# Expert rows scaled on leaving PSUM, both picks gathered with an add onto the h rows, a plain one-hot for the last expert, and rows turned with a column stride

## The chip, the cores and the metric

One NeuronCore of one Trainium2 chip runs one program. The metric is the device time of one execution in microseconds (us). PE is the matrix engine, DVE the vector engine, ACT the scalar engine, POOL the general engine, SP the engine that issues most transfers. Each reads its own instructions in order, and semaphores tie them together.

## The reference

520 tokens (512 of a prompt, 8 samples), 1024 wide, float32. Only the second half of the layer is touched here:

```python
h = layer_norm(ALPHA * x + m, ln1_g, ln1_b)          # m: the token mixer's output
probs = softmax(h @ router_w + router_b)             # 16 experts in 4 groups of 4
# the best group by the sum of its two largest; its two largest are the picks
weights = sel_v / jnp.sum(sel_v, axis=-1, keepdims=True)
for e in range(N_EXPERTS):
    u = jax.nn.silu(t @ w_gate[e]) * (t @ w_up[e])
    out = out + gates[:, e:e + 1] * (u @ w_down[e])
y = layer_norm(ALPHA * h + f, ln2_g, ln2_b)
```

## The kernel before

Every float32 matrix is split in a rounded high part (ACT writes it, for expert weights into `ring`) and a low part (the difference, by POOL for the mixer and by DVE for the experts), and a product is three matmuls: high by high, high by low, low by high. Up to about 690 us the mixer runs so. Then `h` is written to DRAM (`h_rows`) and the experts follow.

An expert takes up to C = 96 tokens. A small product `find_ids` of a one-hot (`mark` on DVE builds it from the token's position in the expert, `posm`) with `id_cols` gives the ids of its tokens, DVE adds them up (`take_ids`), POOL gathers the rows of `h` (`hs`), PE turns them (`turn`, 8 transposes), ACT and DVE split them (`tokens_in`, `tokens_low`). Then come the products gate, up and down, 24 matmuls each. ACT copies the expert's rows out of PSUM (`rows_out`, tile `y_out`) and SP stores them in `y_rows`. Experts are run in the order `TURN`; `each_tile` writes the first and the last three by hand (m = 0, 13, 14, 15) and puts m = 1 to 6 in a loop that runs twice. In the loop DVE, ACT and PE work on three experts at once: in step m PE does gate(m), `find_ids` for m + 2, the turn of u(m-1) and of the rows of m + 1, up(m), down(m-1).

The gate is applied at the end, per token. `h` is loaded back (`h_back`), POOL gathers each token's first pick into `y_a` (the picks in the first 12 experts: `slot_early`) and its second pick into `y_b` (`slot_ready`), and DVE forms `y_a * weight + h_back` (`partial`). Rows of the last expert don't go through DRAM for prompt tokens: PE adds them from `y_last_hi` and `y_last_lo` with a weighted one-hot `share_hi`, `share_lo` (`share_last`), on top of `y_a` that it brings into PSUM by the identity. The 8 sample tokens are spread over 128 partitions (16 per token, 64 wide: `sy_a`, `sy_b`, `sh_back`) and always gathered, so their second gather waits until the last expert's rows are stored (`half_stored`). `results` on DVE then adds `y_b` with its weight, takes mean and variance with ACT (`deviation`) and normalises four blocks of 128 tokens and the samples. In DRAM the rows of `h` lie with even and odd columns apart, so that `turn` reads runs of 128 columns.

A token count over 96 for an expert leads to further passes, behind a branch on `n_max`. These inputs don't take it.

## Time and profile before

| | |
|---|---|
| three runs | 1028.72, 1028.82, 1029.62 us (median 1028.82) |
| the profiled execution | 1029.47 us, of it 1027.7 us span |
| PE, DVE, ACT, POOL busy | 97%, 77%, 47%, 37% |
| mean granted clock of PE | 0.993 |
| mixer, experts, end | to about 690, 714 to 1002, 1002 to 1027.7 us |

The span runs from the first to the last instruction; 1.77 us lie around it. Times in rows are from the span's start.

### The profile page before, as it was taken

What the parts mean: (1) busy time and instruction counts of PE and PEld (TensorE: products, weight loads), DVE (VectorE), ACT (ScalarE), POOL (GpSimd) and SP (SyncE); (2) the same over time, 40 slices, a digit from 0 to 9 for tenths busy, and PEclk for the clock granted to TensorE, in tenths of its full rate; (3) what the DMA queues carried; (4) which work ended last, traced back from release to release, by engine and by line L of the source; (5) the groups of instructions that cost most, each with busy time, mean ns of one, the idle gap of its engine ahead of it and who ended that gap; (6) DMA issues with size and microseconds to landing.
All of it is one profiled execution on the core that took longest, in us unless ns stands there. A gap on an engine that the chain in (4) does not pass through costs nothing.

```text
span 1027.7 us, 19645 instructions
## 1 busy us (share of the span) xinstructions
PE 999.9 (97%) x7246; PEld 904.1 (88%) x7246; DVE 793.4 (77%) x982; ACT 478.5 (47%) x674; POOL 379.0 (37%) x278
## 2 busy tenths in 40 slices
PE   7999999999999999999999999998999999999995
PEld 7999999999999999999999999986677777777773
DVE  4598889888989985844434498237989898999987
ACT  4232322223232335134442323452788887878765
POOL 3444444444454755344544454320200000000355
PEclk9999999999999999999999999998999999999998
DMA  7432323233232222333235522647999999999475
GB/s 219 120 103 82 102 82 97 86 88 95 85 99 82 82 83 73 101 111 91 82 102 162 186 82 92 257 154 286 398 389 397 391 399 389 399 391 399 155 247 179
DMA packets 147290, 190.55 MB, mean 185 GB/s; under 512 B 6819, under 2 KB 114339, under 8 KB 147228
## 3 DMA queue, kind: packets, MB, share of 16 engines
q1 hardware_dynamic: 140107, 176.74, 49.4%
q0 software_dynamic: 3008, 10.55, 3.2%
q10 hardware_dynamic: 4129, 2.67, 0.9%
q8 instruction: 26, 0.43, 0.2%
q14 instruction: 20, 0.16, 0.1%
HBM read 179.16 MB, written 11.76 MB: 186 GB/s over the span
## 4 chain that ended last, share of the span: by engine, by line
PE 91%; DVE 5%; issue 2%; DMA 2%; ACT 1%; POOL 0%; SPq 0%; DVEq 0%; POOLq 0%; ACTq 0%
PE pr L1079 60%; PE pr L1269 16%; PE work L1269 8%; DMA sb_tok<-in_state_conv_b_dram 1%; PE work L1245 1%; PE work L1161 1%; PE pr L1310 1%; PE pr L1289 1%; DMA hs<-h_rows,ids 0%; PE work L1186 0%; DVE y_a L2015 0%; PE work L1087 0%; PE pr L1234 0%; DVE q_hi L1596 0%; PE pr L1178 0%
## 5 line engine op out<-in xcount | busy, mean ns | idle before, releaser
L595 POOL TENSOR_TENSOR w_lo<-raw,w_hi 128x512 fp32r<-128x512 f32 x208 | 297.2, 1449 | 326.8 <-ACT w_hi L724 326.8
L1079 PE MATMUL pr<-x_hi,w_hi 128*128 128x260 f32 x1264 | 255.2, 283 | 0.0
L1079 PE MATMUL pr<-x_hi,w_lo 128*128 128x260 f32 x1264 | 254.8, 283 | 0.0
L1079 PE MATMUL pr<-x_lo,w_hi 128*128 128x260 f32 x1264 | 254.3, 283 | 0.0
L728 ACT ACTIVATE ev<-pr 128x520 f32<-128x520 f32 x96 | 58.2, 606 | 372.7 <-PE pr L1079 372.7
L1079 PEld LDWEIGHTS pr<-x_hi,w_hi 128*128 128x128 f32 x1264 | 195.0, 189 | 0.3
L1079 PEld LDWEIGHTS pr<-x_hi,w_lo 128*128 128x128 f32 x1264 | 194.9, 188 | 0.0
L1079 PEld LDWEIGHTS pr<-x_lo,w_hi 128*128 128x128 f32 x1264 | 194.3, 188 | 0.0
L1522 DVE SCALAR_TENSOR_TENSOR work<-b_pad,par,work 128x512 f32<-128x512 f32 x224 | 148.1, 742 | 0.0
L724 ACT ACTIVATE w_hi<-raw 128x512 fp32r<-128x512 f32 x208 | 118.9, 622 | 3.7 <-DMA raw<-in_w_in_dram 3.4
L632 POOL DMA_INDIRECT hs<-h_rows,ids x15 | 19.3, 1288 | 247.5 <-DVE ids L1801 247.5
L1269 PE MATMUL pr<-ring,hs_hi 128*96 128x512 f32 x246 | 97.8, 398 | 0.0
L1269 PE MATMUL pr<-ring,hs_lo 128*96 128x512 f32 x246 | 96.8, 393 | 0.0
L1705 DVE TENSOR_TENSOR w_up_lo<-w_up,ring 128x1024 fp32r<-128x1024 f32 x64 | 75.2, 1219 | 19.0 <-ACT ring L868 19.0
L868 ACT ACTIVATE ring<-w_gate 128x1024 fp32r<-128x1024 f32 x64 | 67.8, 1062 | 23.3 <-PE pr L1269 10.6
L1705 DVE TENSOR_TENSOR w_down_lo<-w_down,ring 128x1024 fp32r<-128x1024 f32 x64 | 75.3, 1214 | 1.7 <-ACT ring L868 1.7
L1705 DVE TENSOR_TENSOR w_gate_lo<-w_gate,ring 128x1024 fp32r<-128x1024 f32 x64 | 75.4, 1215 | 0.8 <-ACT ring L868 0.7
L1582 DVE TENSOR_TENSOR ev<-ev,ev 128x520 f32<-128x520 f32 x16 | 11.9, 744 | 79.4 <-ACT ev L728 79.4
L868 ACT ACTIVATE ring<-w_down 128x1024 fp32r<-128x1024 f32 x64 | 65.7, 1053 | 4.7 <-PE pr L1269 4.0
L868 ACT ACTIVATE ring<-w_up 128x1024 fp32r<-128x1024 f32 x64 | 62.4, 1046 | 2.1 <-PE pr L1261 1.9
L1269 PEld LDWEIGHTS pr<-ring,hs_lo 128*96 128x96 f32 x246 | 39.7, 161 | 17.3
L1269 PEld LDWEIGHTS pr<-ring,hs_hi 128*96 128x96 f32 x246 | 39.8, 162 | 16.0
(397 smaller groups left out, 1749.7 us busy)
## 6 DMA issues: line engine op xcount, KB each, us to landing
raw<-in_w_in_dram SPq DMA_DIRECT2D x80, 512.0 KB, 3.7
w_gate<-in_expert_w_gate_dram SPq DMA_DIRECT2D x16, 2048.0 KB, 14.4
w_up<-in_expert_w_up_dram SPq DMA_DIRECT2D x16, 2048.0 KB, 13.0
w_down<-in_expert_w_down_dram SPq DMA_DIRECT2D x16, 2048.0 KB, 12.5
y_rows<-y_out SPq DMA_DIRECT2D x14, 384.0 KB
raw<-in_w_a_out_dram SPq DMA_DIRECT2D x8, 512.0 KB, 4.1
raw<-in_w_c_out_dram SPq DMA_DIRECT2D x8, 512.0 KB, 4.1
raw<-in_w_b_out_dram SPq DMA_DIRECT2D x8, 512.0 KB, 3.9
```

The source lines that it names most:

```text
L595: pool.tensor_tensor(w_lo[:, slot, k], raw[:, slot, k], w_hi[:, slot, k].bitcast(F32), ALU.subtract).then_inc(w_split, 1)
L632: pool.indirect_dma_start(out=hs[:], out_offset=None, in_=h_rows, in_offset=bass.IndirectOffsetOnAxis(ap=ids[:, m % 2:m % 2 + 1], axis=0)) ...
L724: act.activation(w_hi[:, slot, k], raw[:, slot, k], ACT.Copy).then_inc(w_rounded, 1)
L728: act.activation(out, src[:, :, 0:HALF], func).then_inc(evacuated, 1)
L868: act.activation(rounded(kind, i, last, opening, slots), chunk(kind, s, i), ACT.Copy).then_inc(ps.hi[kind], 1)
L1079: mm = pe.matmul(pr[slot][:, h, 0:HALF], w[:, slot, k, :], x[:, k, h * HALF:(h + 1) * HALF], start=(k == 0 and w is w_hi and x is hi), sto ...
L1161: mm = pe.matmul(work[TILE[f"sp{q}"]][:, i, c * P:(c + 1) * P], vt[:, c, g * P:(g + 1) * P], ws_t[:, g, :], start=True, stop=True)
L1245: mm = pe.transpose(work[0][:, k // 4, k % 4 * C:(k % 4 + 1) * C], source[:, (k % 2 * 4 + k // 2) * P:(k % 2 * 4 + k // 2 + 1) * P], ident ...
L1269: mm = pe.matmul(out(h), x[:, k, :], w[:, cols], start=(k == 0 and x is hi and w is w_hi_i), stop=(k == k_of * CH - 1 and x is lo))
L1522: do(dve.scalar_tensor_tensor(acc, b_pad[:, k:k + TP], col(j, R_CONVB + k), acc, ALU.mult, ALU.add))
L1582: do(dve.tensor_tensor(gate[:], gate[:], prod[:], ALU.mult))
L1705: dve.tensor_tensor(chunk(kind, s, i, w_e_lo), chunk(kind, s, i), rounded(kind, i, last, opening, slots).bitcast(F32), ALU.subtract).then_ ...
```

## The change

1. **Gate at PSUM.** `find_ids` multiplies the one-hot by `slot_cols`, five columns for each expert: the two of `id_cols` and three bfloat16 parts of the token's weight for that expert. `next_gate` on ACT adds the three parts into a column of `gate`, and `rows_out` copies with `scale=gate`. The gates of the first two experts come from `find_gates` on PE, which takes the place of eight filler transposes (`keep_busy(8)`), and `first_gates` on ACT.
2. **Gathers that add.** Each gather adds its rows to `h_back` in place (`compute_op=ALU.add`), the early one once `h_back` is loaded, the second one once the first has landed (`y_in`). A pick that isn't to be added points at row 0 of `y_rows`, a row of zeros that a new transfer writes near the start. `partial` and all that belongs to it is gone.
3. **Plain one-hot.** `share` is turned and copied once during expert 15 and has no weight and no low part; `share_last` has two matmuls for each half block where it had four, and takes the first halves of blocks 0 to 2 first.
4. **Column stride.** Rows of `h` lie in DRAM in their natural order, and `turn` reads every second column.
5. In `normalised` one dummy Sqrt on ACT moves behind the branch.

The core of the diff (the further pass, renames and declarations left out):

```diff
@@ SP @@
+            sp.wait_ge(x_split, 1)
+            sp.dma_start(y_rows[0:1, :].rearrange("o (a b) -> o a b", b=16), b_pad[0:1, 0:16].unsqueeze(1).to_broadcast([1, D // 16, 16])).then_inc(h_stored, 16)
             sp.dma_start(sb_tok[:], state_conv_b[0].rearrange("(b s) k n -> (s k) b n", b=2)).then_inc(states_in, 16)
@@ POOL @@
+            def fetch(b, slot, table):
+                pool.indirect_dma_start(out=h_back[:, b, :], out_offset=None, in_=table,
+                                        in_offset=bass.IndirectOffsetOnAxis(ap=slot[:, b:b + 1], axis=0), compute_op=ALU.add).then_inc(y_in[b], 16)
...
-            pool.wait_ge(first.done["down"], (E - 1) * CH)
-            fetch(y_a, slot_early, y_a_in, y_rows[0:EARLY * C, :])
-            pool.wait_ge(end_dve, 2)
+            pool.wait_ge(back_in, 32)
+            for b in range(4):
+                fetch(b, slot_early, y_rows[0:EARLY * C + 1, :])
+            pool.wait_ge(end_dve, 3)
...
-                fetch(y_b, slot_ready, y_b_in, y_rows[0:(E - 1) * C, :])
+                for b in range(4):
+                    pool.wait_ge(y_in[b], 16)
+                    fetch(b, slot_ready, y_rows[0:(E - 1) * C + 1, :])
+                pool.wait_ge(y_in[4], 16)
                 pool.wait_ge(first.half_stored, 32)
@@ ACT @@
+            def gate_in(ps, src, m):
+                act.activation(gate_parts[:, m % 2], src, ACT.Copy, accum_out=gate[:, m % 6:m % 6 + 1]).then_inc(ps.gates_in, 1)
+            def first_gates(ps, q):
+                act.wait_ge(ps.gates_mm, q + 1)
+                for j in range(2):
+                    gate_in(ps, pr[1][0:C, 1, 8 + 3 * j:11 + 3 * j], j)
+            def next_gate(ps, m, t):
+                act.wait_ge(ps.ids_ready, t + 4)
+                act.wait_ge(ps.gates_in, t + 2)
+                if m:
+                    act.wait_ge(ps.y_ready, t)
+                gate_in(ps, pr[1][0:C, 1, 2:5], m + 2)
...
                     if m < 15:
                         tokens_in(ps, m + 1, t + 1)
+                    if m <= 13:
+                        next_gate(ps, m, t)
@@ PE @@
-                    mm = pe.matmul(pr[1][0:C, 1, 0:2], onehot[:, b, :], id_cols[:, b, :], start=(b == 0), stop=(b == NTB - 1))
+                    of = id_cols[:, b, :] if x is None else slot_cols[:, b, bass.ds(x, 1), :].rearrange("p o n -> p (o n)")
+                    mm = pe.matmul(pr[1][0:C, 1, 0:2 if x is None else 5], onehot[m % 2][:, b, :], of, start=(b == 0), stop=(b == NTB - 1))
...
-                    mm = pe.transpose(work[0][:, k // 4, k % 4 * C:(k % 4 + 1) * C], source[:, (k % 2 * 4 + k // 2) * P:(k % 2 * 4 + k // 2 + 1) * P], ident[0:C, 0:C])
+                    mm = pe.transpose(work[0][:, k // 4, k % 4 * C:(k % 4 + 1) * C], of_pair[:, k // 2, k % 2, :], ident[0:C, 0:C])
...
                 turn(ps, n0)
-                if ps is first:
-                    keep_busy(8)
+                find_gates(ps, n0)
@@ DVE @@
+                if ps is first:
+                    spread_weights()
...
-                low_parts(ps, "down", 0, t, (3,), last=True)
                 if ps is first:
                     spread_samples()
-                    share_marks()
-                    partials(16)
+                low_parts(ps, "down", 0, t, (3,), last=True)
+                if ps is first:
+                    share_low(0)
+                    share_low(1)
...
-                    step(dve.scalar_tensor_tensor(z_tile[b][:], wide(y_b[:, b, :]), s_wm[:, b:b + 1], z_tile[b][:], ALU.mult, ALU.add,
+                    step(dve.scalar_tensor_tensor(z_tile[b][:], other, 1.0, whole, ALU.mult, ALU.add, accum_out=agg[:, s, 0:1]))
```

How the instructions stand on an engine, at the three places that the prediction speaks of. First ACT, from the last chunk of the first expert's gate matrix on. Before:

```order
L868 ACTIVATE ring<-w_gate_74 128x1024 [waits first_gate_in0,h_stored]
L891 ACTIVATE hs_hi<-work 128x768 [waits first_turned]
L868 ACTIVATE ring<-w_up_77 128x1024 [waits first_gate_done,first_up_in0]
L868 ACTIVATE ring<-w_up_77 128x1024 [waits first_gate_done]
L922 ACT_TABLE_LOAD [waits first_u]
```

With the change:

```order
L875 ACTIVATE ring<-w_gate_74 128x1024 [waits first_gate_in0,h_stored]
L905 ACTIVATE gate_parts,gate<-pr 96x3 [waits first_gates_mm]
L905 ACTIVATE gate_parts,gate<-pr 96x3
L898 ACTIVATE hs_hi<-work 128x768 [waits first_turned]
L875 ACTIVATE ring<-w_up_77 128x1024 [waits first_gate_done,first_up_in0]
```

Two small instructions, with a wait on PE's `find_gates`, now stand ahead of the rows' high part. Second PE in the loop, between gate and the turn of u. Before:

```order
L1231 REGISTER_ALU
L1234 MATMUL pr<-id_cols,onehot 96x2 [waits first_ids_ready,first_onehot]
L1234 MATMUL pr<-id_cols,onehot 96x2 x4
L1308 ISA
L1310 MATMUL pr<-ident,u 128x96 [waits first_u]
```

With the change:

```order
L1259 REGISTER_ALU
L1263 ISA [waits first_ids_ready,first_onehot]
L1263 MATMUL pr<-slot_cols,onehot_183 96x5
L1263 ISA
L1263 MATMUL pr<-slot_cols,onehot_183 96x5
L1263 ISA
L1263 MATMUL pr<-slot_cols,onehot_183 96x5
L1263 ISA
L1263 MATMUL pr<-slot_cols,onehot_183 96x5
L1263 ISA
L1263 MATMUL pr<-slot_cols,onehot_183 96x5
L1347 ISA
```

The wait moved from a matmul to a register instruction ahead of it (ISA: it computes the address of the expert's columns), and each of the five matmuls has such an instruction. Third ACT at the end, the two halves of the last expert's rows. Before:

```order
L907 ACTIVATE y_last<-work 96x512 [waits first_down_done]
L911 ACTIVATE share_hi<-pr 96x512 [waits end_mm]
L912 ACTIVATE y_last_hi<-work 96x512
L914 DMA y_rows<-y_last 96x512 [waits first_half_ready]
L907 ACTIVATE y_last<-work 96x512 [waits first_down_done]
L912 ACTIVATE y_last_hi<-work 96x512
L914 DMA y_rows<-y_last 96x512 [waits first_half_ready]
```

With the change:

```order
L934 ACTIVATE y_last_hi<-work,gate 96x512 [waits first_down_done,first_gates_in]
L936 ACTIVATE y_last<-work,gate 96x512 [waits end_dve]
L938 DMA y_rows<-y_last 96x512 [waits first_half_ready]
L934 ACTIVATE y_last_hi<-work,gate 96x512 [waits first_down_done]
L936 ACTIVATE y_last<-work,gate 96x512 [waits end_dve]
L938 DMA y_rows<-y_last 96x512 [waits first_half_ready]
```

`y_last`, which is what gets stored, is now written last of the two, after DVE has formed the low part (`end_dve`).

## Rows read from the trace of the kernel before

**Rows 1.** The page: span, and the chain that ended last by engine.

```profile
span 1027.7 us, 19645 instructions
PE 91%; DVE 5%; issue 2%; DMA 2%; ACT 1%; POOL 0%; SPq 0%; DVEq 0%; POOLq 0%; ACTq 0%
```

**Rows 2.** The chain in order of time (start, us, what), one expert apart.

```profile
929.13 0.18 PE pr L1234 x5
...
947.00 0.18 PE pr L1234 x5
```

**Rows 3.** The same chain near the start.

```profile
15.22 0.39 SPq L425
...
15.65 11.39 DMA sb_tok<-in_state_conv_b_dram
```

**Rows 4.** Timeline, first expert (start, us, engine, line, operation, [idle before <-releaser]).

```profile
711.96 1.14 PE L1245 MATMUL work<-ident,hs 96*128 96x96 f32 x8 [0.24 <-DMA hs<-h_rows,ids]
...
713.14 0.81 ACT L891 ACTIVATE hs_hi<-work 128x768 fp32r<-128x768 f32 x1 [8.51 <-PE work L1245]
```

**Rows 5.** Timeline, ACT: the smallest reading of PSUM with a sum.

```profile
1016.31 0.31 ACT L1001 ACTIVATE y_b<-pr,s_agg 128x64 f32<-128x64 f32 x1
```

**Rows 6.** Timeline, one expert of the loop.

```profile
941.56 1.02 ACT L900 ACTIVATE y_out<-work 96x1024 f32<-96x1024 f32 x1 [1.78 <-PE work L1269]
...
945.84 0.65 DVE L1794 TENSOR_TENSOR onehot<-ev,router 128x480 bf16<-128x480 f32 x1
...
946.84 0.34 PE L1234 MATMUL pr<-id_cols,onehot 128*96 128x2 bf16 x5
```

**Rows 7.** Line 1794: register instructions of DVE (x, min/median/max ns).

```profile
L1794 DVEq FUSED_REGOPS  x12: 64/64/81, 729.4 to 926.7; - x12
```

**Rows 8.** Timeline, the same expert, further on (DVE).

```profile
950.95 0.15 DVE L1801 TENSOR_REDUCE ids<-pr 96x1 int32<-96x2 f32 x1
```

**Rows 9.** Timeline, the last expert's products and rows.

```profile
998.37 0.16 DVE L1942 COPY s_spread<-pr 128x5 f32<-128x5 f32 x1
...
999.99 0.64 PE L1374 MATMUL pr<-ident,share_tok 128*96 128x128 f32 x4 [0.48 <-DVE share_tok L1955]
...
1002.05 0.59 ACT L907 ACTIVATE y_last<-work 96x512 f32<-96x512 f32 x1 [0.31 <-PE work L1302]
...
1002.68 0.32 ACTq L914 DMA_DIRECT2D y_rows<-y_last  x1
...
1004.07 0.68 DVE L1977 TENSOR_TENSOR y_last_lo<-work,y_last_hi 96x512 fp32r<-96x512 f32 x1
```

**Rows 10.** Timeline, POOL's second gathers and DVE after them.

```profile
1000.83 1.74 POOL L677 DMA_INDIRECT y_b<-y_rows,slot_ready  x1 [0.82 <-DVE slot_ready L1961]
...
1008.30 2.02 POOL L682 DMA_INDIRECT y_b<-y_rows,s_idx  x1 [0.30 <-issue]
...
1006.76 1.29 DVE L2006 SCALAR_TENSOR_TENSOR pr<-y_b,s,pr 128x1024 f32<-128x1024 f32 x1 [0.82 <-PE pr L1387]
...
1008.22 1.27 DVE L1967 SCALAR_TENSOR_TENSOR y_a<-y_a,s,h_back 128x1024 f32<-128x1024 f32 x1
...
1014.65 1.28 DVE L2015 SCALAR_TENSOR_TENSOR y_a<-work,agg,ln_rows 128x1024 f32<-128x1024 f32 x1
```

**Rows 11.** Transfers issued in 1000 to 1002.5, 1002.5 to 1005 and 1008 to 1012 us (last: us to landing).

```profile
y_rows<-y_last ACTq DMA_DIRECT2D x1, 192.0 KB, 2.1
...
y_b<-y_rows,slot_ready POOLq DMA_INDIRECT x1, 5.5
...
y_rows<-y_last ACTq DMA_DIRECT2D x1, 192.0 KB, 4.2
...
y_b<-y_rows,s_idx POOLq DMA_INDIRECT x1, 4.6
```

**Rows 12.** Busy time by stretch (PE, PEld, DVE, ACT, POOL, granted clock, DMA share, GB/s).

```profile
706.00:712.00 6.00, 4.95 (x29) 4.47 (x28) 2.58 (x16) 0.00 (x0) 2.02 (x2) 0.50 0.43 130
...
1003.00:1012.00 9.00, 8.99 (x28) 5.14 (x29) 7.96 (x12) 6.04 (x9) 6.41 (x4) 1.00 0.84 259
```

More of the change, by code:

```diff
@@ L265, in build @@
         u_lo = place("u_lo", "par", [P, FB, C], F32R)
-        onehot = place("onehot", "acc_a", [P, NTB, C], BF16)
+        onehot = [place(f"onehot{i}", "acc_a", [P, NTB, C], BF16, plus=i * NTB * C * 2) for i in range(2)]
+        slot_cols = place("slot_cols", "rw", [P, NTB, E, 5], BF16)
         iota = ev[4][:, 0:C]
@@ L324, in build @@
         more_posm = sem("more_posm")
[L325 to L326 removed]
+        y_in = [sem(f"y_in{b}") for b in range(NTB)]
+        cols_ready = sem("cols_ready")
         y_read = sem("y_read")
@@ L553, in _ @@
                 sp.wait_ge(first.half_stored, 32)
-                sp.wait_ge(partial_ready, NTB)
+                for b in range(NTB):
+                    sp.wait_ge(y_in[b], 16)
                 sp.wait_ge(end_mm, 6)
@@ L1351, in step @@
                     if m <= 13:
-                        find_ids(ps, t + 2)
+                        find_ids(ps, m, t + 2, expert(2))
                     if m:
@@ L1384, in part @@
                     cols = slice(h * D // 2, (h + 1) * D // 2)
-                    pe.matmul(z_tile[b][:, h, :], ident[:], y_a[:, b, cols], start=True, stop=False)
-                    for w, y in ((share_hi, y_last_hi), (share_lo, y_last_hi), (share_hi, y_last_lo)):
-                        mm = pe.matmul(z_tile[b][:, h, :], w[:, n], y[:, cols], start=False, stop=y is y_last_lo)
-                    return mm
-                pe.wait_ge(end_dve, 5)
-                pe.wait_ge(partial_ready, 1)
-                part(0, 0)
-                pe.wait_ge(end_dve, 6)
-                part(0, 1).then_inc(end_mm, 1)
-                for b in (1, 2, 3):
-                    pe.wait_ge(partial_ready, b + 1)
-                    part(b, 0)
-                    part(b, 1).then_inc(end_mm, 1)
+                    for y in (y_last_hi, y_last_lo):
+                        mm = pe.matmul(z_tile[b][:, h, :], share[:, n], y[:, cols], start=y is y_last_hi, stop=y is y_last_lo)
+                    return mm
+                for h in range(2):
+                    pe.wait_ge(end_act, 2 + h)
+                    pe.wait_ge(end_dve, 4 + h)
+                    for b in range(3):
+                        mm = part(b, h)
+                        if h:
+                            mm.then_inc(end_mm, 1)
+                pe.wait_ge(first.half_ready, 2)
+                part(3, 0)
+                part(3, 1).then_inc(end_mm, 1)
             pe.sem_inc(first.turned, 1)
@@ L1964, in partial @@
-            def partial(b, landed):
-                dve.wait_ge(y_a_in[b], landed)
-                to = y_a[:, b, :] if landed == 16 else z_tile[b][:].rearrange("p h t -> p (h t)")
-                dve.scalar_tensor_tensor(plain(to), plain(y_a[:, b, :]), s_wa[:, b:b + 1], paired(h_back[:, b, :]), ALU.mult,
-                                         ALU.add).then_inc(partial_ready, 1)
-            def sample_partial(landed):
-                dve.wait_ge(y_a_in[4], landed)
-                dve.scalar_tensor_tensor(plain_s(sy_a), plain_s(sy_a), s_spread[:, 3:4], paired_s(sh_back), ALU.mult, ALU.add).then_inc(partial_ready, 1)
```

257 lines of the change are left out of this document (118 added, 139 removed).

## The prediction

> **What bounds the kernel now.** I read the page first: PE holds 91% of the chain that ended last, DVE 5% [rows 1]. The chain in order of time then shows what that means for an expert: the same group of five small matmuls returns after 17.87 us (947.00 less 929.13), and between the two the chain never leaves PE [rows 2]. So in the loop any time that PE loses is lost, and nothing that DVE, ACT or POOL save is gained. Two stretches are different. At the start the chain runs through SP: a weight load is issued at 15.22, `sb_tok` 0.43 us later, and its landing releases PE [rows 3]. When the first expert begins, ACT stands 8.51 us until the first rows are turned, and PE's first gate matmul hangs on ACT's high part [rows 4]. At the end, from 1002 us, PE has little to do, and DVE, ACT, the gathers and the last stores set the pace [rows 9, 10].
>
> The change works at all of these places, so I go through it in order of time. Its sum is made against the profiled execution, 1029.47 us, which is 0.65 above the median of the three runs, 1028.82; I add the sum to the median.
>
> **The zero row.** SP issues one more transfer between the weight load and `sb_tok`. Neighbours in that queue stand 0.43 us apart [rows 3], it is on the chain, and PE has no slack behind it: **+0.45 us** (0.3 if it issues like a small one, 0.7 if 64 pieces of 64 bytes take longer than one plain block).
>
> **The first two gates.** `find_gates` can't start before the turn (PE in order); its inputs on DVE, nine small operations after the second ids, end while the rows are still on their way, since ACT has 8.51 us of waiting there [rows 4]. Ten small matmuls take twice a group of five (0.18 us in the chain, 0.34 with the last one's end [rows 2, 6]), some 0.45 us; they replace eight fillers, so PE issues no more than before. But ACT now waits for them and then does two readings with a sum before `hs_hi`. The nearest row is 0.31 us for 64 columns [rows 5]; three columns may take 0.25. 0.4 + 2 x 0.27 = **+0.95 us** on the path to the first gate matmul (0.7 to 1.3). What follows is paced by PE and moves with it.
>
> **In the loop, PE.** `find_ids` keeps five matmuls with five columns in place of two; nothing by itself. But its columns are now found by a register, and ahead of each of the five stands a register instruction; the first of them holds the wait for the one-hot, so PE's sequencer stops there instead of running ahead. The one-hot is ready at 946.49 (945.84 + 0.65), 0.35 us before PE takes the group up at 946.84 [rows 6]. `y_out`, now with a scale from memory, may add up to 0.1 to ACT and so to the one-hot, which stands behind ACT's `ring` for up. A register instruction for the same purpose took DVE 64 ns [rows 7]. Five of them, with 0.04 us for each matmul (0.18 / 5), are 0.5 us from 946.55, so the last matmul goes out at about 947.05 where before all five had gone at 947.02, and the turn of u waits for one register instruction more. At 64 ns I get some 0.1 us lost, at twice that 0.35. No row shows PE's own register instructions. I take 0.15 for each of twelve looped experts: **+1.8 us**, bounds 0 (the sequencer is fast enough) and 4.2.
>
> **In the loop, the rest.** ACT gets `next_gate`, about 0.3 us, and has to wait for DVE's ids (951.1 [rows 8]), about 1.2 us later than it would come to it. ACT sits 1.78 us before `y_out` in every expert [rows 6] and also waits for PE between the chunks of `ring`, so it has caught up by then: **0**, and up to +0.2 per expert if that cover is gone. `y_out` needs the gate two experts later: no wait. The turn reads columns 8 bytes apart. No row has PE reading so; the nearest is DVE, whose operations on `y_a` with every second column took 1.27 us against 1.28 and 1.29 for plain ones [rows 10]. I take **0**; if the turn took half as long again (eight in 1.14 us, at a clock not yet full [rows 4]), 16 experts would add 9 us.
>
> The Trainium skill ("SBUF — State Buffer", section "Door 1: The DMA port swizzle") says that memory is read in lines of 16 bytes, at full rate with at least two hits in a line, which four-byte elements at a step of two still have. By it the turn costs nothing, the same as my 0.
>
> **Expert 15.** The four transposes of the one-hot, with the 0.48 us that PE waited for DVE [rows 9], leave the space between the last products; the transposes come back before `up_last`, with a copy of 0.6 us on ACT ahead of the store and the last down chunks, and the samples' indices (0.35 us from 998.37) now stand ahead of DVE's last low part. About 0.9 goes and 0.75 comes: the last product ends as before, near 1002 us, and the first half 0.9 later than before.
>
> **The last store.** Per half ACT writes `y_last_hi` (0.59), DVE `y_last_lo` (0.68), then ACT `y_last` (0.59) and its store [rows 9]. ACT is through with the first half at about 1002.8, and with the second 2.0 later: the second store goes out at 1004.75 instead of 1002.68. Stores of this form took 2.1 and 4.2 us [rows 11]; with gathers beside it I take 4.2: landed at 1009.0.
>
> **The gathers.** The samples' index no longer waits behind the one-hot's arithmetic, so the second gathers start at about 999.8 instead of 1000.83 [rows 10], if the early ones have landed. The first lands 5.5 us later [rows 11], 1005.3; PE, with eight matmuls less in front, is ready by 1004.8. DVE then starts adding at 1005.3 instead of 1006.76, and needs the samples 7.9 us less two partials (1.27 and 0.3) later, at 1011.5. But the samples' second gather waits for the last store, 1009.0 (before it began at 1008.30), and takes 4.6 us [rows 10, 11]: 1013.6, and the block after it starts at 1013.85 instead of 1014.65. What follows is as before. **-0.8 us**, bounds: -3.1 if the samples are not late, -0.1 if the store is 0.7 slower. One table load less on ACT lies beside DVE's work and gives nothing.
>
> A gather that adds must read `h_back` too. No row has one. Below: nothing extra. Above: twice the time of the engines. I take **+0.5**.
>
> **The sum:** 0.45 + 0.95 + 1.8 - 0.8 + 0.5 = +2.9 us, so 1028.82 + 2.9 = **1031.7 us**.
>
> **Rivals.**
>
> *Register instructions are covered.* If PE's sequencer loses nothing in the loop, the sum is +1.1: 1029.9 us. For it: other register instructions already stand in PE's loop, some with a wait, and the chain shows PE without a gap [rows 2]. Against: the wait now stops the sequencer, 0.35 us before the matmuls are due.
>
> *The adding gathers double.* From 1003 to 1012 the transfer engines are busy 84% [rows 12]. If adding rows double that work, 7.6 us become about 13, and the samples land near 1017 instead of 1013: +3.4 on the forecast's other terms, 1034.6 us with the loop's loss and 1032.8 without. The Trainium skill ("Collectives: The Full Stack", section "The bandwidth ceiling: the fold count and why AG ≠ RS ≠ AR") says that a reduce in the transfer engines costs two source reads and so halves the rate. That rule speaks against the change, and would give this case; no run here shows it yet. The early gathers, which begin only once `h_back` is in, would also end later.
>
> *Faster.* If the last store lands in 2.1 us, the samples are gathered right behind the other rows and DVE is the bound: -3.1 at the end. Adding is free and the register instructions are covered: 0.45 + 0.95 - 3.1 = -1.7, 1027.1 us. It decides at the samples' landing: only before about 1011.5 us, and with the head's 1.4 us cut to under 1, is the kernel faster by over 0.2%.
>
> *The clock.* PE ran at half its clock (1.2 GHz) from 706 to 712 us, after little work [rows 12]. The new 1.4 us gap behind the turn may bring that back: a third of an expert (one product, 17.87 / 3 = 6 us [rows 2]) at half clock costs 6 us more, of which 2 to 5 would show: 1034 to 1037.
>
> *The column stride costs PE*, as above: 1041.
>
> **How the numbers follow.** 0.2% (2.1 us) is about what can be told from no change. The forecast, a loss in the loop of 0.05 to 0.35 per expert with gathers that cost little: 0.36. Covered registers, gathers cheap: 0.26. Doubled gathers: 0.14. Clock or stride: 0.08. Faster end: 0.16, of which about 0.13 beyond 0.2% when I count what no row shows. Slower by over 0.2% (above 1030.9) is two thirds of the first, most of the doubled ones and the clock, a fifth of the second, 0.52; the same 0.34; faster 0.14. The range reaches from the faster end to the doubled gathers: 1027.0 to 1035.0.
>
> **What would show it.** The start of `sb_tok`'s issue at 16.1 instead of 15.65; ACT's `hs_hi` of the first expert 1.4 us after the turn's end rather than at once; one expert of the loop at 18.0 instead of 17.87 us; the stride: time from `find_ids` to the up product grown by more than the register instructions explain; the second half's store at 1004.8 relative to a last product at 1002; the landing of gathers near 5.5 us. I would be wrong above all if PE's loop period doesn't move, if the adding gathers take much longer than plain ones, or if the samples are no longer what DVE waits for.

## The result: 1.7% slower

| kernel | median of its runs | ratio to before |
|---|---|---|
| before, beside it | 1029.22 us (4 runs, 1028.72 to 1029.88) | |
| changed | 1046.71 us (4 runs, 1045.62 to 1047.37) | 1.0168, 95% interval 1.0151 to 1.0186 |

The forecast was 1031.7 us in a range that ended at 1035.0. The loss is 17.5 us of medians, and 17.9 us between the two profiled spans (1045.6 and 1027.7 us). Between the profiled spans it came in three stretches: about 3.7 us at the start of the first expert and the turn behind it (the forecast had 0.95 there), 9.6 us from the first looped expert to the last expert's first product (it had 1.8), and 5.7 us behind the last product (it had 0.3 less than before). Expert 15 gained 0.8 us, and the first turn began 0.4 us earlier.

The first lines of the page of the changed kernel; PE holds the chain almost as before (90% and 91%, [rows 1]):

```profile
span 1045.6 us, 19709 instructions
PE 90%; DVE 4%; issue 3%; DMA 1%; ACT 1%; POOL 0%; ACTq 0%; SPq 0%; DVEq 0%; POOLq 0%
```

### The profile page after: what moved, and what is told of

Its sections match the earlier page's. It is cut to its first block, busy times and chain, and to the rows that moved or that the text cites. A ratio compares the mean times of both kernels' runs of the same rounds, so it can differ in the third digit from the quotient of the medians.

```text
span 1045.6 us, 19709 instructions
## 1 busy us (share of the span) xinstructions
PE 1003.2 (96%) x7224; PEld 909.4 (87%) x7224; DVE 791.8 (76%) x969; ACT 478.1 (46%) x703; POOL 368.0 (35%) x278
## 4 chain that ended last, share of the span: by engine, by line
PE 90%; DVE 4%; issue 3%; DMA 1%; ACT 1%; POOL 0%; ACTq 0%; SPq 0%; DVEq 0%; POOLq 0%
PE pr L1107 59%; PE pr L1308 16%; PE work L1308 8%; PE work L1284 1%; DMA sb_tok<-in_state_conv_b_dram 1%; PE work L1189 1%; PE pr L1263 1%; PE pr L1349 1%; PE pr L1328 1%; DMA hs<-h_rows,ids 0%; PE work L1214 0%; DVE y_a L2024 0%; PE work L1115 0%; DVE q_hi L1635 0%; PE pr L1206 0%
## 5 line engine op out<-in xcount | busy, mean ns | idle before, releaser
L631 POOL DMA_INDIRECT hs<-h_rows,ids x15 | 13.9, 929 | 265.8 <-DVE ids L1853 250.7
L1308 PEld LDWEIGHTS pr<-ring,hs_lo 128*96 128x96 f32 x246 | 40.0, 162 | 17.5
```

The lines of the kernel that those rows point to most:

```text
L631: pool.indirect_dma_start(out=hs[:], out_offset=None, in_=h_rows, in_offset=bass.IndirectOffsetOnAxis(ap=ids[:, m % 2:m % 2 + 1], axis=0)) ...
L1308: mm = pe.matmul(out(h), x[:, k, :], w[:, cols], start=(k == 0 and x is hi and w is w_hi_i), stop=(k == k_of * CH - 1 and x is lo))
```

## The profile after

**The loop.** The chain in order of time (start, us, what), one expert apart. It answers to [rows 2]:

```profile
922.11 0.50 PE pr L1263 x5
922.61 0.51 PE pr L1349 x4
923.11 0.96 PE work L1284 x8
924.07 5.56 PE pr L1308 x24
929.63 5.52 PE work L1308 x24
935.15 5.56 PE pr L1308 x24
940.71 0.51 PE pr L1263 x5
```

An expert takes 940.71 less 922.11, 18.60 us, where it took 17.87. The three products are as before. What grew stands between gate and up: the five small matmuls of `find_ids` (L1263) take 0.50 where they took 0.18, the turn of u behind them (L1349) 0.46 to 0.51, where it took 0.39 us, and the turn of the rows (L1284, the column stride) 0.96 where it took 0.66. Twelve experts lose 8.8 us, and the turns of experts 13 and 14 another 0.6.

Two more kinds of rows say where in these groups the time goes. They list the instructions of one line over the whole run (min/median/max in ns). PE loads one operand of each matmul before it runs (PEld, LDWEIGHTS). Before, for the turn:

```profile
L1245 PEld LDWEIGHTS work<-ident,hs x120: 139/141/230, 712.0 to 965.5; 96*128 96x128 f32 x120
```

With the change, for the turn and for the register instructions of `find_ids`:

```profile
L1284 PEld LDWEIGHTS work<-ident,hs x120: 195/216/218, 711.5 to 978.4; 96*128 96x128 f32 x120
L1263 PEldq FUSED_REGOPS  x60: 46/46/84, 735.5 to 940.9; - x60
```

Each load of the turn takes 216 ns instead of 141, and each of the 60 register instructions (5 in each of 12 experts) 46 ns.

**The first expert.** Its timeline (start, us, engine, line, operation, idle time before it and releaser) answers to [rows 4]:

```profile
711.54 1.20 PE L1284 MATMUL work<-ident,hs 96*128 96x96 f32 x8 [1.01 <-DMA hs<-h_rows,ids]
712.58 0.57 PE L1272 MATMUL pr<-slot_cols,onehot 128*96 128x3 bf16 x10
713.19 0.17 ACT L905 ACTIVATE gate_parts<-pr 96x3 f32<-96x3 f32 x1 [8.79 <-PE pr L1272]
713.50 0.80 ACT L898 ACTIVATE hs_hi<-work 128x768 fp32r<-128x768 f32 x1
714.35 0.74 PE L1296 MATMUL pr<-ring,hs_hi 128*96 128x512 f32 x1 [1.20 <-ACT hs_hi L898]
714.89 0.63 PE L1297 MATMUL pr<-w_gate_lo,hs_hi 128*96 128x512 f32 x1
```

The first product starts 2.81 us after the start of the turn; before it was 2.04 (the chain in the kernel before has the turn at 711.96 and L1257 at 714.00). And the matmuls behind it come 0.43 us apart (714.89 to 715.32, say), where they came 0.23 apart. The busy times of three stretches (PE, PEld, DVE, ACT, POOL, granted clock, DMA share, GB/s) give the reason; of before only 706 to 712 stands in [rows 12], and its granted clock from 716 to 720 was 1.00:

```profile
706.00:712.00 6.00, 4.44 (x27) 4.20 (x28) 4.32 (x22) 0.00 (x0) 2.09 (x2) 0.72 0.48 145
712.00:716.00 4.00, 2.80 (x21) 2.27 (x20) 1.67 (x2) 1.11 (x5) 0.00 (x0) 0.66 0.46 83
716.00:720.00 4.00, 4.00 (x10) 2.51 (x10) 4.00 (x5) 1.24 (x2) 0.00 (x0) 0.50 0.97 395
```

PE's granted clock is 0.50, its lower level (1.2 GHz), until 720 us, after it stood idle 1.0 us before the turn and 1.2 us behind the small matmuls. (By single microseconds it is 1.00 from 710 to 713 and 0.50 from 714 on.) So the first gate product costs 2.6 us more: 8.40 us from its start to the next `find_ids` (714.35 to 722.75) instead of 5.85 (714.00 to 719.85). Its last 18 matmuls in the chain:

```profile
717.22 5.53 PE pr L1308 x18
```

This price isn't the same in every execution. Eight of the profiled kernels have no fillers there (the changed one and kernels 2, 3 and 6 to 10 below), all with the gap of 1.2 us ahead of the product, and it takes 8.40, 7.1 to 7.9 and, in kernel 2, 5.87 us: there the granted clock stayed at 1.00. With four or eight fillers (six profiles, that of before among them) it takes 5.6 to 5.9.

**The end.** The last product ends at 1014.20 us, and the span 31.4 us later; in the kernel before it was 1002.02 and 25.7 us. ACT's timeline:

```profile
1012.91 0.69 ACT L934 ACTIVATE y_last_hi<-work,gate 96x512 fp32r<-96x512 f32 x1 [2.94 <-PE work L1341]
1014.41 0.69 ACT L936 ACTIVATE y_last<-work,gate 96x512 f32<-96x512 f32 x1 [0.82 <-DVE y_last_lo L2003]
...
1017.72 0.32 ACTq L938 DMA_DIRECT2D y_rows<-y_last  x1
1026.32 1.28 ACT L1049 ACT_TABLE_LOAD   x1 [8.63 <-issue]
1027.61 0.20 ACT L1049 ACTIVATE r_tok<-eps_t 1x1 f32<-1x1 f32 x1
1027.72 1.09 ACT L1011 ACTIVATE y_b<-pr,agg 128x1024 f32<-128x1024 f32 x1
```

ACT stands 8.63 us behind its last store, in which it waits for nothing that a semaphore shows ("issue"); before it stood 2.89 us ahead of its first instruction behind the branch (L981), and was through in time. (A table load and the Sqrt of L1012 stood ahead of the branch then; from the issue of the last store to the first instruction behind the branch it was 4.5 us, and now 8.3.) POOL and DVE in the same stretch, which answers to [rows 10]:

```profile
1001.77 1.66 POOL L675 DMA_INDIRECT h_back<-y_rows,slot_early  x1 [31.82 <-DMA h_back<-h_rows]
...
1026.17 1.55 POOL L680 DMA_INDIRECT h_back<-y_rows,s_idx  x1 [5.60 <-DMA y_rows<-y_last]
```

```profile
1021.68 1.23 DVE L2016 SCALAR_TENSOR_TENSOR pr<-pr,h_back 128x1024 f32<-128x1024 f32 x1 [4.71 <-DMA h_back<-y_rows,slot_ready]
...
1025.04 1.23 DVE L2016 SCALAR_TENSOR_TENSOR work<-work,h_back 128x1024 f32<-128x1024 f32 x1 [1.88 <-DMA h_back<-y_rows,slot_ready]
...
1029.01 1.28 DVE L2024 SCALAR_TENSOR_TENSOR y_a<-pr,agg,ln_rows 128x1024 f32<-128x1024 f32 x1 [2.50 <-ACT y_b L1011]
...
1036.40 1.23 DVE L2049 SCALAR_TENSOR_TENSOR y_b<-h_back,s_agg 128x64 f32<-128x64 f32 x1
...
1037.74 2.19 DVE L2052 SCALAR_TENSOR_TENSOR y_a<-y_b,s_agg,h_back 128x64 f32<-128x64 f32 x1
```

Three things are seen. The early gathers start at 1001.8, when `h_back` is in, where they were over long before; DVE waits 4.71 and 1.88 us for the second ones. Then it waits 2.50 us for ACT. And two operations on 64 columns take 1.23 and 2.19 us. The last transfers' rows in 1013 to 1016 us, where nothing but adding gathers ran:

```profile
q0 software_dynamic: 163, 0.60, 105.7%
...
h_back<-y_rows,slot_ready POOLq DMA_INDIRECT x2, 9.7
```

A landing takes 9.7 us instead of 5.5 [rows 11]. In 3 us 16 engines, busy all the time, moved 0.60 MB: 5.3 us of all engines per MB. In the kernel before, in 1004 to 1008 us, the row of the same queue (packets, MB, share of the 16 engines' time) gives 3.1 us per MB:

```profile
q0 software_dynamic: 266, 0.97, 75.4%
```

The last store of `y_last` is later too: it is issued 3.5 us behind the last product (1017.72 and 1014.20), where it was 0.7 (1002.68 and 1002.02), and lands some 8 us after that; the samples' gather waits 5.60 us for it.

## The experiments

All ratios are to the kernel before, measured beside it (medians 1028.7 to 1029.0 us). Each interval reaches 0.9 to 1.6 us to either side. The part up to the first expert varies by 3.5 us between executions (the first one-hot at 704.2 to 707.7 us in the profiles of these kernels), so stretches of the traces say more than medians where a us is at stake. They have a scatter as well: behind the last product the changed kernel and kernels 2 to 5, which have the same end, take 30.7 to 31.4 us, and the kernel before and kernel 1 25.7 and 25.5.

**1. The stride alone, on the kernel before** (with the loads of `h_back` and DVE's sums in natural order to match):

```diff
+                of_pair = source[:].rearrange("s (j p i) -> s j i p", p=P, i=2)
...
-                    mm = pe.transpose(work[0][:, k // 4, k % 4 * C:(k % 4 + 1) * C], source[:, (k % 2 * 4 + k // 2) * P:(k % 2 * 4 + k // 2 + 1) * P], ident[0:C, 0:C])
+                    mm = pe.transpose(work[0][:, k // 4, k % 4 * C:(k % 4 + 1) * C], of_pair[:, k // 2, k % 2, :], ident[0:C, 0:C])
```

> The kernel before with the column stride alone: rows of h in natural order, the turn reads every second column. Theory A (the stride costs PE in loading the columns): in the changed kernel eight transposes of a turn took 0.96 us in the chain, and 0.66 before, also where no register instruction is near (experts 13 and 14, not looped). So each of 16 turns grows by 0.3 us, the loop's period goes from 17.87 to about 18.17 us, and the time from 1029.2 to about 1033.9 (+4.7). Rival B (my prediction: the stride is free, and the longer turn in the changed kernel came from something else in it): period 17.87, time within 1 us of before.

Measured: 1036.79 us, 1.0071 (1.0058 to 1.0084). The chain has the turn at 0.96 us:

```profile
918.10 0.18 PE pr L1232 x5
918.28 0.39 PE pr L1309 x4
918.67 0.96 PE work L1244 x8
...
936.28 0.18 PE pr L1232 x5
```

The period is 18.18 us: the stride costs 0.3 us a turn, and my zero falls. The time rose by 7.8 us, where 4.7 was expected. The other 3 us of this kernel lie in one place, before the loop's second turn:

```profile
753.20 1.19 PE L1244 MATMUL work<-ident,hs 96*128 96x96 f32 x8 [1.94 <-DMA hs<-h_rows,ids]
```

The gather for it took POOL 8.65 us to issue (6.31 in the kernel before, 0.92 for most), its rows landed late, and PE's clock fell for the product behind.

**2. The stride taken out of the changed kernel.** Rows stay in natural order and the turn reads runs of 128 columns, so the columns of h meet the rows of the weights in another order. The diff is that of kernel 1, backwards and nothing else:

```diff
-                of_pair = source[:].rearrange("s (j p i) -> s j i p", p=P, i=2)
```

> The changed kernel with the turn reading runs of 128 columns; rows still lie in natural order, so the columns of h meet the rows of the weights in another order: the amount of work, the routing and all waits stay. Theory A (the stride costs each turn 0.3 us and nothing else; the kernel before with the stride lost 2.9 us more, in one late gather of the rows of the third expert, which is a matter of when that gather meets the weight loads): the loop's period goes from 18.60 to 18.28 us and the time falls by 4.5 to 5 us, to about 1042. Rival B (the stride costs nothing in the changed kernel, its turn being long for the register instructions): period and time unchanged. Rival C (the stride has a second price of some 3 us): the time falls by 7.5 us, to 1039.

Measured: 1041.60 us, 1.0132 (1.0117 to 1.0146), 5.1 us less than the changed kernel. The turn is 0.66 us again, the period 18.3 (733.66 to 752.02 us, the turns of u). By the period the stride costs 0.3 us a turn, 4.5 us in fifteen, and the late gather was an extra of kernel 1. Why it is late there wasn't found. The rest can't be put down to the stride, for in this kernel's profile the first product ran at full clock, without a filler and behind the same gap (1.2 us, up to 714.53):

```profile
716.23 4.17 PE pr L1307 x18
```

How often that happens in its other executions isn't known.

**3. The five columns at a fixed address.**

```diff
-                    of = id_cols[:, b, :] if x is None else slot_cols[:, b, bass.ds(x, 1), :].rearrange("p o n -> p (o n)")
+                    of = id_cols[:, b, :] if x is None else slot_now[:, m % 2, b, :]
@@ DVE, mark @@
+                if cols:
+                    dve.tensor_copy(slot_now[:, m % 2], slot_cols[:, :, bass.ds(x, 1), :].rearrange("p b o n -> p b (o n)"))
```

> The changed kernel, but DVE copies the expert's five columns to a fixed tile ahead of each one-hot, so that PE's five small matmuls need no register instruction. Theory A (register instructions cost PE 0.33 us at the small matmuls and about 0.07 at the turn of u behind them): the five take 0.18 us in the chain again instead of 0.50, the loop's period goes from 18.60 to about 18.2 us, and the time falls by 4.0 to 4.9 us, to about 1042. Rival B (five columns in place of two, or where they lie, is what costs): the period stays at 18.6. Rival C (the DVE copy, some 0.15 us more ahead of the one-hot, makes PE wait): period between.

Measured: 1041.68 us, 1.0122 (1.0107 to 1.0136), 5.0 us less. Same five matmuls, same five columns, no register instruction:

```profile
917.53 0.19 PE pr L1264 x5
917.72 0.39 PE pr L1350 x4
918.10 0.95 PE work L1285 x8
...
935.72 0.19 PE pr L1264 x5
```

18.19 us, 0.41 less than 18.60. Rivals B and C are out: DVE's copy, 0.16 us, is hidden. In its profile the first product takes 7.36 us, 1.0 less than in the changed kernel's, so a part of the 5.0 us may be the clock's; the period's 0.41 times twelve gives 4.9.

**4. Fillers in the gap.**

```diff
                 find_gates(ps, n0)
+                if ps is first:
+                    keep_busy(8)
```

> The changed kernel with eight filler transposes again, behind the first two gates' matmuls and ahead of the first gate product. Theory A (the gap of 1.2 us ahead of the first product brought the clock of PE down to 0.50 for 716 to 720 us): with fillers in the gap the granted clock from 716 to 720 is 1.00 again, the first products take 0.23 us each, and the time falls by 2.5 to 3 us, to about 1044. Rival B (the gap of 1.0 us before the turn, with fewer fillers behind, decides it): clock still 0.50 in that stretch, time unchanged.

Measured: 1043.92 us, 1.0151 (1.0136 to 1.0166), 2.8 us less. That is as Theory A said, though the two intervals of the ratio overlap; the trace is clearer. The granted clock from 716 to 720 us is full, with 24 matmuls where there were 10, and the first product takes 5.86 us instead of 8.40:

```profile
716.00:720.00 4.00, 4.00 (x24) 2.84 (x23) 4.00 (x5) 3.30 (x4) 0.00 (x0) 1.00 1.02 419
```

**5. Fillers, and the gates read behind the high part.**

```diff
@@ ACT @@
-                first_gates(ps, q)
...
                         tokens_in(ps, 0, t)
+                        first_gates(ps, q)
@@ PE @@
+                    if m == 0:
+                        pe.wait_ge(ps.gates_in, t + 2)
                     if m <= 13:
                         find_ids(ps, m, t + 2, expert(2))
```

> The changed kernel with the eight fillers (1043.9 us alone) and with ACT reading the first two gates behind the rows' high part, not ahead of it. Theory A (the first two gates cost the path what the chain showed: 0.43 us on PE and 0.41 us on ACT): the high part starts at the end of the turn, the fillers follow find_gates, and the first product starts about 0.8 us earlier relative to the turn: 1043.1 us. Rival B (the fillers, 0.9 us behind find_gates, end later than the high part, and PE in order makes the first product wait for them): gain 0.2 us or less, to be read in PE's row of the first product: no idle ahead of it.

Measured: 1044.72 us, 1.0153 (1.0140 to 1.0167), which is no gain on kernel 4 (0.8 us more by the medians, within the scatter). From the turn to the first product it is 2.55 us (712.26 to 714.81), against 2.82 in kernel 4. Rival B holds: in the chain the first product starts where the last of eight fillers ends, at 714.81. The mixed kernel (11) has four.

**6. Gathers that don't add.** The sums of h and the first picks are left out with it.

```diff
-                                        in_offset=bass.IndirectOffsetOnAxis(ap=slot[:, b:b + 1], axis=0), compute_op=ALU.add).then_inc(y_in[b], 16)
+                                        in_offset=bass.IndirectOffsetOnAxis(ap=slot[:, b:b + 1], axis=0)).then_inc(y_in[b], 16)
```

> The changed kernel with gathers that write over h_back in place of adding to it: it leaves out the sums of h and the first picks (the output is then the last picks alone, normalised), with all waits, counts and bytes written as they are. Theory A (an adding gather costs the transfer engines 1.7 times a plain one, 5.3 us of all engines per MB instead of 3.1): landing of the second gathers falls from about 10 us to near 6, the stores of the last rows land in 3 to 5 us instead of 8, ACT's code is there earlier than 1026.3, and the time falls by 5 to 7 us, to about 1040 to 1042. Rival B (adding costs nothing; the gathers are late because they wait for h_back): landing stays near 10 us and the time within 1 us of the changed kernel.

Measured: 1044.98 us, 1.0152 (1.0139 to 1.0165), only 1.7 us less where 5 to 7 was expected. The landing falls to 6.6 us as expected, and DVE sums the first block at 1018.6; but then

```profile
1027.00 1.28 DVE L2024 SCALAR_TENSOR_TENSOR y_a<-pr,agg,ln_rows 128x1024 f32<-128x1024 f32 x1 [4.76 <-ACT y_b L1011]
```

it waits for ACT, which comes at 1024.3. From the last product to the end it is 28.9 us: 2.5 less than in the changed kernel, 1.8 less than the shortest of the five equal ends.

**7. No branch on ACT**: its part of the further pass, which these inputs don't take, is left out.

```diff
-            n_max = further_passes(act)
-            with act.If(n_max > C):
...
-            with act.Else():
-                act.nop()
             act.activation(r_tok[0:1, 0:1], eps_t[0:1, 0:1], ACT.Sqrt)
```

> The changed kernel without ACT's part of the further pass, which these inputs don't take, and so without ACT's branch: its code runs straight on. Theory A (ACT stood 8.63 us at the end because code behind a taken branch has to be fetched, and the fetch queues behind the adding gathers): ACT takes up its table load right behind the last store, near 1018, the first deviation runs as soon as DVE has its sum (1023.2) and not at 1027.7, DVE's idle 2.50 us ahead of the first normalising goes, and the time falls by 2 to 2.5 us (then DVE waits for gathers). Rival B (ACT waited for something else, such as its store's landing at about 1026): ACT still starts near 1026, time unchanged.

Measured: 1045.19 us, 1.0167 (1.0153 to 1.0181).

```profile
1017.44 0.32 ACTq L938 DMA_DIRECT2D y_rows<-y_last  x1
1017.79 1.28 ACT L1040 ACT_TABLE_LOAD   x1 [0.38 <-ACT y_last L936]
```

The same table load comes 0.4 us behind the store, not 8.6. So ACT waited for what the branch brings, not for the store's landing, which is as late here (POOL's gather behind it starts at 1026.3). From the last product to the end it is 29.3 us: 2.1 less, 1.4 less than the shortest equal end. By the medians it is 1.5 less, where 2 to 2.5 was expected. That the wait is a fetch of code is the likeliest reading: in all twelve profiled kernels with ACT's branch a packet of the queue q14, of kind instruction, moves in the half microsecond that ends 1.5 us before ACT goes on, and in this kernel and the next there is none in that place. The traces don't show more directly what ACT waits for, nor why the packet comes later beside adding gathers.

**8. Both 6 and 7**, by the same two diffs.

> Both: gathers that write over h_back (the sums of h and first picks are left out), and no branch on ACT. With plain gathers alone the first sums on DVE ran at 1018.6 and 1020.8 but ACT came at 1024.3, so that only 1.7 us were gained. Theory A (adding costs 1.7 times the transfer engines' time, and what it costs was hidden behind ACT's late code): now DVE normalises from about 1022.5, and waits next for the samples, whose gather waits for the last store (landed 1024.5) and lands near 1029; the time falls by 4 to 5 us against the changed kernel, to about 1042, more than the two alone. Rival B (the two add up: 1.7 plus what the missing branch gives).

Measured: 1043.17 us, 1.0142 (1.0127 to 1.0158). The end takes 26.9 us, 4.5 less, where 2.5 and 2.1 make 4.6: the two add up (rival B), within the scatter of such ends, and I had expected more than the sum. By the medians it is 3.5 less. What is late next is the samples' gather, behind a last store that takes some 7 us to land: DVE stands 2.96 us for it at 1027.6.

**9. The samples through PSUM.**

```diff
+                do(dve.tensor_copy(pr[0][:, 0, 0:CS], sh_back))
...
-                do(dve.scalar_tensor_tensor(sy_a, sy_b, s_agg[:, 3:4], sln2[:, 1, :], ALU.mult, ALU.add), to_fin)
+                do(dve.scalar_tensor_tensor(sy_a, pr[0][:, 0, 0:CS], s_agg[:, 3:4], sln2[:, 1, :], ALU.mult, ALU.add), to_fin)
```

> The changed kernel, with the samples' two last operations on DVE taking one operand from PSUM (one small copy more) in place of both from SBUF. Theory A (an operation of DVE with both operands in SBUF can't run beside POOL's additions; both took until POOL's end, 1.23 and 2.19 us, where the kernel before, with one operand in PSUM, took 0.28 each beside the same additions): they take 0.3 us each, the last block's normalising starts at about 1038.1 in place of 1039.85, the time falls by 1.7 us to about 1045. Rival B (the 64 columns of h_back or the tile y_b are slow for another reason, such as a wait for ACT): the durations stay at 1.2 and 2.2 us, time unchanged.

Measured: 1046.26 us, 1.0174 (1.0160 to 1.0188): by the medians nothing, where 1.7 us was expected. The trace shows the mechanism:

```profile
1034.87 0.28 DVE L2050 SCALAR_TENSOR_TENSOR pr<-pr,s_agg,h_back 128x64 f32<-128x64 f32 x1
...
1035.25 0.28 DVE L2053 SCALAR_TENSOR_TENSOR y_a<-pr,s_agg,h_back 128x64 f32<-128x64 f32 x1
...
1036.29 1.29 DVE L2024 SCALAR_TENSOR_TENSOR work<-work,agg,ln_rows 128x1024 f32<-128x1024 f32 x1 [0.76 <-ACT y_b L1011]
```

0.28 us each, beside POOL's additions (4.65 us for two from 1033.5), and the last block's normalising comes 1.9 us earlier behind the last product. But from the first of the two operations to the end of the span it is 8.4 us, where the changed kernel and kernels 2 to 6 have 9.1 to 9.3: 0.7 less. The output's last transfers now go out together and land in 3.4 us instead of 2.3.

**10. The gathers and the rows of the kernel before.** Pairs in DRAM again, plain gathers into `y_a` and `y_b`, DVE adding `h_back` without a weight. With them come back ACT's order at the end (`y_last` and its store ahead of `y_last_hi`), the samples' operand in PSUM and the order of `share_last`. Gate at PSUM, zero row, plain one-hot and the moved Sqrt stay. The core of its diff:

```diff
+            def partial(b, landed):
+                dve.wait_ge(y_in[b], landed)
...
+                dve.scalar_tensor_tensor(plain(to), plain(y_a[:, b, :]), 1.0, paired(h_back[:, b, :]), ALU.mult,
+                                         ALU.add).then_inc(partial_ready, 1)
...
+                    pe.matmul(z_tile[b][:, h, :], ident[:], y_a[:, b, cols], start=True, stop=False)
```

> The changed kernel with rows of h paired as before and the turn reading runs of columns, and with the gathers of the kernel before: plain ones into y_a and y_b, DVE adding h_back to y_a without weights, PE bringing it into PSUM by the identity. What stays of the change: the gate at PSUM, the zero row, the plain one-hot, the moved Sqrt. Theory A: the loop at 18.28 us (register instructions 0.41 in 12 experts, 4.9), the start with its half clock (2.8) and gates (0.8), and the end as long as before, 25.7 us from the last product, or 0.5 to 1 shorter (one table load, twelve matmuls and a few operations on DVE fewer): 1029 + 4.9 + 2.8 + 0.8 - 0.5 = about 1037. Rival B (the end is long for the gate at PSUM or for the branch, not for the gathers): the end stays above 30 us and the time near 1042.

Measured: 1034.89 us, 1.0058 (1.0045 to 1.0071). The profiled execution was 3.2 us above the median (1038.14 us), most of it ahead of the first expert, whose one-hot comes at 707.66. The end takes 24.9 us, 6.5 less than in the changed kernel and 0.8 less than before, which is as Theory A has it; the period is 18.29 us. The gate at PSUM and the plain one-hot don't make the end longer. The estimate of 1037 was 2 us too high, and what this kernel paid for the clock in its profile was 1.6 us, not 2.8.

**11. The same with every price taken out** (the diffs of kernels 3 and 5, with `keep_busy(4)` for `keep_busy(8)`).

> The same with the columns of an expert copied to a fixed tile by DVE, four fillers behind find_gates, and ACT reading the first gates behind the rows' high part: every price found so far undone. Theory A: the loop's period is 17.87 us again, the start as before (within 0.3 us), the end 0 to 1 us shorter than before: 1028 to 1029 us, the same as before. Rival B (the gate at PSUM costs something in the loop that the other prices hid, such as ACT's or DVE's extra operation): period above 17.9 and the time above 1030.

Measured: 1027.87 us, 0.9995 (0.9985 to 1.0004; 12 runs). The chain:

```profile
931.25 0.19 PE pr L1270 x5
931.44 0.39 PE pr L1355 x4
931.82 0.66 PE work L1290 x8
...
949.10 0.19 PE pr L1270 x5
```

17.85 us, the period of before: the scale on `y_out`, `next_gate` and DVE's copy cost nothing. The end takes 24.8 us. It is no faster than before beyond what the runs can tell: Theory A.

**12. One of DVE's sums moved ahead** in kernel 11.

```diff
                 partial(0, landed)
+                partial(1, landed)
                 share_low(0)
-                partial(1, landed)
                 share_low(1)
```

> The mixed kernel with DVE's second sum of y_a and h_back moved ahead of the low part of the last expert's first half, into the 1.30 us that DVE stood there. Theory A (the end is paced by ACT, which has its code 4.3 us late behind the branch and starts the first deviation at 1011.2 in its profile): the first sum with y_b starts 0.5 us earlier, but the first normalising doesn't, and the time stays within 0.3 us of the mixed kernel, 1027.9. Rival B (the end is paced by DVE and PE from the last products on): 0.5 us less, 1027.4, beyond doubt under the kernel before.

Measured: 1028.42 us, 0.9993 (0.9984 to 1.0002). No gain: DVE was ready and stood 2.45 us for the first rows of `y_b`, and ACT 5.79 us behind its branch. The end isn't DVE's to shorten by this order. Theory A has the size right; of its cause the trace shows ACT, and a gather beside it.

## Why the prediction was wrong

Of six causes that it mis-sized or left out it named four: the register instructions (at a third of their size), the adding gathers (a rival with a chance of 0.14), the clock and the stride (0.08 together). It didn't name ACT's branch or the samples' operands. The steps that failed worst are the end, the stride and the loop's register instructions. Going by all its steps, with the share of the 17.9 us in the profiled spans:

- **The zero row, +0.45.** `sb_tok` is issued at 16.04 us (I had said 16.1), its transfer taking 0.67 us on SP. It doesn't show in the time: the first one-hot comes at 704.62, 0.5 earlier than in the profile of before, inside the scatter of that stretch.
- **The first two gates, +0.95.** From the turn's start to the first product 0.77 us more: right.
- **The clock, 0.08 together with the stride.** It happened, with 2.6 us in the profiled execution, in the lower half of "2 to 5", and with 0 to 2.0 in seven other profiles with the same gap; what decides it isn't shown. I had the gap, and the stretch at half clock before it, but took the eight fillers for idle filling ("PE issues no more than before") and not for what can keep the clock up until the product. That was the step: a filler has no duration to save, and a gap at its place has a price.
- **The loop, PE: +1.8.** The mechanism was right, the term mis-sized: 0.41 us for each of twelve, 5.0 by kernel 3. The step that failed is the overlap. I had the group of five at 0.5 us, and it takes 0.50; but I let it begin at 946.55, when the one-hot is ready, though PE is in gate's last matmul until 946.84 by the same rows. Begun there it ends 0.3 later than before, and 0.50 - 0.18 = 0.32 is what the chain shows; another 0.07 or more goes at the turn of u. (PE's register instruction took 46 ns and not DVE's 64; a matmul with one ahead took 0.10 us all the same.) At its "at twice that 0.35" the working was near the measured size, but I took 0.15.
- **The loop, ACT: 0.** Right. ACT waits 1.31 us for the ids ahead of `next_gate` and catches up.
- **The column stride: 0.** Wrong, 0.3 us in each of 15 turns, about 4.5. The row from which I argued was DVE's, and PE's load isn't like it (216 ns instead of 141). The bound of 9 us had the right form, each turn half as long again, but took it of 1.14 us, a turn mostly at half clock, where the loop's take 0.66. The Trainium skill's rule ("SBUF — State Buffer", section "Door 1: The DMA port swizzle"), lines of 16 bytes at full rate with two hits in each, agreed with my zero; with a step of two elements PE's turn takes 0.96 us against 0.66, so here the measurement decides against it.
- **Expert 15.** "The last product ends as before": it saved 0.8 us (from the start of its gate product to the last product 24.3 instead of 25.1).
- **The end, -0.8 and +0.5.** This step failed worst: 5.7 us longer instead of 0.3 shorter. I had the samples' gather, behind the last store, as what DVE waits for; it waited 4.71 and 1.88 us for the second gathers and 2.50 for ACT instead, and not for the samples. The adding gathers cost 1.7 times a plain one's engine time, near the rival's double, and landed in 9.7 us. The Trainium skill ("Collectives: The Full Stack", section "The bandwidth ceiling: the fold count and why AG ≠ RS ≠ AR") has two source reads and half the rate for the reduce step of a collective; the trace goes the same way, with 1.7 in place of 2. But by kernel 6 it is only 2.5 us of the end, since DVE then waits for ACT in its place. The second part, 2.1 us, is ACT behind its branch, which I left out, though the trace of before has 2.89 us of "issue" there. The third, 1.9 us at DVE and 0.7 in the end, is the samples' operations, which lost their operand in PSUM. I counted operations and not where their operands lie. The Trainium skill has that rule ("SBUF — State Buffer", section "SBUF: two separate sides"): an operation of DVE with two inputs in SBUF and one of POOL that reads SBUF exclude each other, and the other waits till the first is through. The trace agrees: POOL's additions (4.65 us for two from 1035.20) end at 1039.85 us, and DVE's operation behind L2052 starts at 1039.85.

The three parts of the end are 5.3 of its 5.7 us, each known to some 0.7 us at best. The rest wasn't taken apart, and neither was a rival: ACT's new order, which issues the last store 2.8 us later, was undone in kernels 10 to 12 only, together with the gathers. In sum 2.6 + 0.8 at the start with 0.3 for its second turn and -0.4 ahead of it, 9.6 from the first looped `find_ids` to the last expert's gate product (254.25 us against 244.65), -0.8 in expert 15 and 5.7 at the end: 17.8 of 17.9 us.

## What to carry to other kernels

Where an engine is the bound for 90% of the span, cost each instruction that you put on it, register instructions and longer operand reads included, at full price times its count, unless a row shows that very engine hiding it: twelve times 0.41 us and fifteen times 0.3 were over half of this loss. A filler ahead of a wait, a PSUM operand, and slack behind a branch are resources that the time table doesn't show: look what held the place before you reuse it. And two transfers chained by an add trade one engine's cheap work for the busiest resource at the end.

## What the runs showed of the hardware

- PE: ahead of each of five matmuls a register instruction (46 ns) for an operand's address, with a wait on the first, cost 0.32 us, and 0.07 or more at the next group.
- PE: eight transposes of 96 by 128 from every second float32 column took 0.96 us, from plain ones 0.66; one load took 216 ns instead of 141.
- PE: behind a gap of 1.2 us the first gate product took 7.1 to 8.4 us in seven profiles, with the granted clock at 0.50 for part of it, and 5.87 in an eighth, where the clock stayed full; with fillers in the gap 5.6 to 5.9 in six.
- A gather that adds took 5.3 us of all 16 engines per MB, a plain one 3.1, and POOL 1.55 us to issue against 0.94 (kernel 6).
- ACT stood 7.9 to 8.6 us at its branch beside adding gathers, 4.9 to 6.1 beside plain ones, 2.8 and 2.9 where a table load and a Sqrt stood ahead of the branch, and 0.4 us without the branch.
- DVE: 64 columns with both operands in SBUF took 1.2 and 2.2 us beside POOL's additions, and 0.28 each with one in PSUM (kernel 9).
- One gather of 96 rows took POOL 0.9 us to issue in most places and 6.3 to 8.7 in one, with 3 us lost behind it in kernel 1. What decides that stays open.
